# Latent queries, keys and values computed with tokens on partitions, heads turned by TensorE, and a new order of the portions between the heads

## What is computed

```python
q = (rmsnorm(c_q, g_cq) @ w_uq).reshape(B, S, MLA_HEADS, MLA_QK)          # 384 -> 8 heads x 96
kv = (rmsnorm(c_kv, g_ckv) @ w_ukv).reshape(B, S, MLA_HEADS, MLA_NOPE + MLA_V)   # 256 -> 8 x (64 + 64)
k_nope, v = kv[..., :MLA_NOPE], kv[..., MLA_NOPE:]
k = jnp.concatenate([k_nope, k_rope], axis=-1)       # k_rope: 32 features, the same for all heads
q = rmsnorm(q, g_qn)
k = rmsnorm(k, g_kn)
q = concat([q[..., :64], apply_rope_2(q[..., 64:], cos, sin)]); k likewise
return dense_attention(q * (MLA_QK ** -0.5), k, v)   # softmax over 256 keys
```

## Time and profile before

| | |
|---|---|
| median of 3 runs | 1648.69 us (1645.78 to 1649.99) |
| the profiled execution | 1644.55 us |
| its span | 1642.8 us |
| mean granted clock of TensorE in it | 0.995 |
| PE busy | 1589.0 us (97%) |
| DVE, ACT busy | 1129.8 us (69%), 919.0 us (56%) |

### The profile page before, as it was taken

The page is one execution under the profiler, slowest core; times in us unless marked ns, Lnnn a source line. Parts: engine busy times, 40 slices in busy tenths (PEclk is TensorE's granted clock), DMA queues, the critical chain, the costliest instruction groups (busy, mean ns, idle before and its releaser), DMA issues. The chain is left out here.

```text
span 1642.8 us, 31046 instructions
## 1 busy us (share of the span) xinstructions
PE 1589.0 (97%) x12874; PEld 1463.2 (89%) x12874; DVE 1129.8 (69%) x1763; ACT 919.0 (56%) x1459; POOL 127.2 (8%) x106
## 2 busy tenths in 40 slices
PE   6999999999999999999999999999999999999999
PEld 3987478999999999966899999878999998799999
DVE  2799677645566655897765556778887567788873
ACT  3444756545365444647554446767666467676662
POOL 0230000112001100300011000000101000001110
PEclk9999999999999999999999999999999999999999
DMA  9443666656546555435566653323555533245553
GB/s 395 160 152 131 258 236 227 235 216 240 192 167 221 205 188 201 155 125 207 195 228 237 220 184 119 118 78 130 207 191 202 204 112 116 77 137 200 207 193 118
DMA packets 46172, 303.36 MB, mean 185 GB/s; under 512 B 5072, under 2 KB 7376, under 8 KB 12752
## 3 DMA queue, kind: packets, MB, share of 16 engines
q1 hardware_dynamic: 45312, 299.78, 50.7%
q0 software_dynamic: 288, 0.92, 0.1%
q10 hardware_dynamic: 432, 0.68, 0.1%
HBM read 298.22 MB, written 3.15 MB: 183 GB/s over the span
## 5 line engine op out<-in xcount | busy, mean ns | idle before, releaser
L2002 DVE TENSOR_TENSOR wl<-raw,wh 128x1040 fp32r<-128x1040 f32 (+1 forms) x472 | 576.4, 1260 | 295.8 <-ACT wh L1759 229.9
L1759 ACT ACTIVATE wh<-raw 128x1040 fp32r<-128x1040 f32 (+1 forms) x472 | 466.5, 1031 | 195.5 <-PE bank L1552 109.3
L1547 PE MATMUL bank<-hx_hi,wh 128*128 128x256 f32 x1856 | 519.6, 280 | 6.0 <-ACT hx_hi L1759 3.8
L1552 PE MATMUL bank<-hx_lo,wh 128*128 128x256 f32 x1856 | 516.2, 278 | 0.0
L1550 PE MATMUL bank<-hx_hi,wl 128*128 128x256 f32 x1856 | 514.7, 277 | 0.3 <-DVE wl L2002 0.2
L1547 PEld LDWEIGHTS bank<-hx_hi,wh 128*128 128x128 f32 x1856 | 349.0, 188 | 10.8 <-issue 9.8
L1550 PEld LDWEIGHTS bank<-hx_hi,wl 128*128 128x128 f32 x1856 | 349.1, 188 | 2.8 <-issue 1.7
L1552 PEld LDWEIGHTS bank<-hx_lo,wh 128*128 128x128 f32 x1856 | 348.8, 188 | 1.0 <-DVE hx_lo L1995 0.4
L1550 PE MATMUL bank<-hid_hi,wl 128*128 128x256 f32 x912 | 252.2, 277 | 1.4 <-DVE wl L2002 1.4
L1547 PE MATMUL bank<-hid_hi,wh 128*128 128x256 f32 x912 | 252.5, 277 | 0.3 <-ACT wh L1759 0.2
L1552 PE MATMUL bank<-hid_lo,wh 128*128 128x256 f32 x912 | 251.9, 276 | 0.0
(11 more groups left out here) (218 smaller groups left out, 1891.5 us busy)
## 6 DMA issues: line engine op xcount, KB each, us to landing
raw<-in_wts SPq DMA_DIRECT2D x208, 1032.0 KB, 4.9
raw<-in_wts SPq DMA_DIRECT2D x50, 1024.0 KB, 6.6
raw<-in_wts SPq DMA_DIRECT2D x20, 776.0 KB, 4.3
raw<-in_wts SPq DMA_DIRECT2D x4, 584.0 KB, 4.4
tscr<-tmp SPq DMA_DIRECT2D x4, 512.0 KB, 7.4
bias<-tscr SPq DMA_DIRECT2D x4, 512.0 KB, 6.0
raw<-in_wts SPq DMA_DIRECT2D x2, 648.0 KB, 4.0
xTc<-in_ctxT SPq DMA_DIRECT2D x1, 1024.0 KB, 10.6
```

The source lines that it names most:

```text
L1547: pe.matmul(out, block(f, M.wh, w0 + k, ncols, c, m), x_hi, start=first and k == 0 and o == 0, stop=False, skip_group_check=True)
L1552: ins = pe.matmul(out, block(f, M.wh, w0 + k, ncols, c, m), x_lo, start=False, stop=last and k == nk - 1, skip_group_check=True)
L1759: return act.activation(out, in_, func, bias=bias, scale=scale)
L2002: tt(M.wl[k][:, cols], M.raw[r][:, cols], M.wh[k][:, cols].bitcast(F32), ALU.subtract).then_inc(*on.inc(lo))
```

## The change

Four parts, for both layers of the second block.

1. **Queries.** Tokens go on partitions: `mla_q` multiplies `cqn` (128 tokens, stationary) by `w_uq` (384 columns, four heads), nine matmuls for each of two token blocks and two halves of the heads: Q0, Q1 are the token blocks of heads 0 to 3, Q2, Q3 of heads 4 to 7. ACT squares 128x384 and copies the 64 plain features; DVE rotates the 32 others with short operations and sums the squares per head. The rest, `qn2`, is four transposes on PE (128x96 to 96x128), root on ACT, and a copy to `q2` with the gain.
2. **Keys and values.** `w_ukv` is stored with all key columns ahead of all value columns. K0, K1 are the two token blocks (six matmuls of 512 columns each). ACT squares 512 columns, DVE sums per head; the first rest (`mla_k2`) takes the root on eight columns and scales by four DVE products; it puts a second rest on `pending` (`mla_k3`: eight transposes, two copies to `k2` with the gain). V is as before, and is now what gives `ukv` back.
3. **Tables.** Sine and cosine are made as 128x32 and not 96x256, and twelve small operations (`rope_rows`) multiply the gains in. `swap2` and a column of constants go away, POOL's `lora1` memset too; the shared key part is turned by two 32-column transposes, rotated and its squares summed.
4. **The table of portions.**

```diff
-BETWEEN = ("h r D0 h L0 L2 N r r D2 D4 r D3", "", "D1 r r Q0", "K0", "", "s K1 h s V Q1", "r r", "s r D5 h h", "h r",
-           "Q3 Q2 h", "", "s K2 r r r K3 h", "s", "r O0 h O1 s", "", "O2", "", "h O3 h", "h", "h s T0 T1 T2 T3 h")
+BETWEEN = ("h r D0 h D2 r L0 r", "L2 N D4", "D3 r", "D1 r r K0", "s K1 r", "Q0 r r", "Q1 r r h h", "r D5 h", "V h",
+           "Q2 h h", "Q3 r h", "r O0 h", "O1 s", "h", "O2 h", "h", "O3 h", "h", "h", "h s T0 T1 T2 T3 h")
```

The core of the rest:

```diff
 TensorE
-    def qn2(s, s_free, r, r_free, sq, t_sq, xg, t_xg, t_s, t_r, **_):
-        for j in range(4):
-            ins = mm(s.t[:, j:j + 1], sq.t[0:96, P * j:P * j + P], M.ones[0:96, 0:1], j == 0, True)
-        mm(r.t[0:96, :], M.swap2[0:96, 0:96], xg.t[0:96, :], True, True).then_inc(*on.inc(t_r))
+    def mla_q(f, tb, b, free, cq_toks, t):
+        out, sl = b.t[:, 0:384], slice(P * tb, P * tb + P)
+        for k in range(3):
+            mm(out, M.cqn[0][:, k, sl], block(f, M.wh, k, 384, 0, 384), k == 0, False)
+            mm(out, M.cqn[0][:, k, sl], block(f, M.wl, k, 384, 0, 384), False, False)
+            ins = mm(out, M.cqn[1][:, k, sl], block(f, M.wh, k, 384, 0, 384), False, k == 2)
+    def heads_turned(o, y):
+        for i in range(4):
+            ins = pe.transpose(o.t[0:96, P * i:P * i + P], y.t[:, 96 * i:96 * i + 96], M.ident)
+    def mla_kv(f, c0, tb, b, ck_toks):
+        for k in range(2):
+            c = slice(1024 * k + c0, 1024 * k + c0 + 512)
+            mm(b.t[:, :], M.ckn[0][:, k, sl], M.wh[f["k"]][:, c], k == 0, False)
+            mm(b.t[:, :], M.ckn[0][:, k, sl], M.wl[f["k"]][:, c], False, False)
+            ins = mm(b.t[:, :], M.ckn[1][:, k, sl], M.wh[f["k"]][:, c], False, k == 1)
-    def mla_k2(sq, x, nb, nb_free, tn, **_):
-        mm(nb.t[0:96, :], M.ones[0:96, 0:96], sq.t[0:96, :], True, True).then_inc(*on.inc(tn))
+    def mla_k3(ys, ready, os, free, ts, **_):
+        for i in range(2):
+            heads_turned(os[i], ys[i]).then_inc(*on.inc(ts[i]))
 VectorE
+    def rope_on(dst, w, src, C, S, t):
+        tt(w[0], src, C, ALU.mult)
+        tt(w[1][:, :, 0:16], src[:, :, 16:32], S[:, :, 0:16], ALU.mult)
+        tt(w[1][:, :, 16:32], src[:, :, 0:16], S[:, :, 16:32], ALU.mult)
+        tt(dst, w[0], w[1], ALU.add)
+    def mla_k2(tb, b, d, ys, y_free, t_krr, t_r, t_y, **_):
+        for i in range(2):
+            tt(y[:, :, 0:64], b.t[:, T * i:T * i + T].rearrange("p (h c) -> p h c", c=64), r.to_broadcast([P, 4, 64]), ALU.mult)
+            tt(y[:, :, 64:96], M.krt[:, tb, :].unsqueeze(1).to_broadcast([P, 4, 32]), r.to_broadcast([P, 4, 32]), ALU.mult)
 Plan
+        def latent(part):
+            if not ukv:
+                ukv.append(take(("ukv", l), look=False))
+            t = mla_values(ukv[0]) if part == "V" else keys(int(part), ukv[0])
+            n_kv.append(t)
+            if len(n_kv) == 3:
+                p.done(ukv[0], t)
```

More of the change, by code:

```diff
@@ L85, in shape_constants @@
     c["swap1"] = j1
[L86 to L91, removed]
+    sq = np.concatenate([c[k] for k in ("ident", "ones", "bones", "swap1")], axis=1)
     t = np.arange(T)
@@ L218, in __init__ @@
         b1_off = cur[0]
-        self.ident, self.ones, self.bones, self.swap1, self.swap2 = (
-            cst[:, P * i:P * i + P] for i in range(5))
+        self.ident, self.ones, self.bones, self.swap1 = (
+            cst[:, P * i:P * i + P] for i in range(4))
         self.V = lambda k: vec[:, VT[k][0]:VT[k][0] + VT[k][1]]
@@ L1149, in tables @@
         t, t_l = ev("mm"), ev("tab")
-        t_d = [ev("tab") for _ in range(18)]
+        t_d = [ev("tab") for _ in range(19)]
         t_sin = [ev("sin"), ev("sin")]
@@ L1156, in tables, with rope_rows @@
         small["t_l"] = t_l
-        tmps.give(small["rb"], t_d[0], t)
-        tmps.give(angb, t_d[-1])
         tmps.give(kb, t_d[-1])
-        t_rope[:] = [t_sin[1]]
+        small.update(ang=angb, t_sin=t_sin, t=t)
+    def rope_rows():
+        t_g = [ev("tab") for _ in range(12)]
+        step("rope_rows", ang=small["ang"], rb=small["rb"], t_sin=small["t_sin"], t_rw=small["t_rw"], b1_free=b1_free,
+             t_g=t_g)
+        tmps.give(small["rb"], t_g[-1], small["t"])
+        tmps.give(small["ang"], t_g[-1])
+        t_rope[:] = [t_g[-1]]
     def copy_out(i):
@@ L1281, in lora_norm @@
             pending.append(rest)
-        q_toks, k_toks, v_toks, qs_toks = [], [], [], []
+        q_toks, k_toks, v_toks, qs_toks = [[], []], [[], []], [], [[], []]
         uq = []
[L1287 to L1294, removed]
@@ L1456, in rest @@
                 pending.pop(0)()
-        portion = {"r": rest, "s": p.one, "h": p.one_half, "V": lambda: mla_values(ukv[0])}
+        portion = {"r": rest, "s": p.one, "h": p.one_half, "V": lambda: latent("V")}
         portion.update({f"D{j}": (lambda j=j: hfree.update(x=[dil_piece(j)])) for j in range(6)})
@@ L1933, in lora2 @@
             fn(dst, us[c][0].t[:, 0:T], ACT.Copy).then_inc(*on.inc(c_toks[c][0]))
+        on.wait_ge(t_sw, y1_free)
+        fn(y1.t[:, 128:192], br.t[:, 0:64], ACT.Square).then_inc(*on.inc(t_k2))
     def mla_v(j, b, t, x, rf, **_):
@@ L2500 @@
     lams = np.stack([i[k] for k in ("lambda_q1", "lambda_k1", "lambda_q2", "lambda_k2")], axis=1)
+    rows = np.concatenate([np.float32(10000.0) ** (-np.arange(16, dtype=np.float32) / np.float32(16))]
+                          + [i[f"g_mla_{k}_2"][l][64:96] for l in range(2) for k in "qk"]).astype(np.float32)
     arrays = {
```

358 lines of the change are left out of this document (195 added, 163 removed).

## The result

| | before | after |
|---|---|---|
| median of the runs | 1648.3 us (4 runs, 1645.8 to 1650.0) | 1693.4 us (4 runs, 1692.4 to 1694.4) |
| ratio, 95% interval | 1 | 1.0275, 1.0257 to 1.0293 |
| span of the profiled execution | 1642.8 us | 1692.6 us |
| first head gemm to head 8's maximum, layers 0 and 1 | 81.06 and 81.06 us | 96.02 and 98.09 us |
| from there to the end of the last value product | 41.94 and 41.95 us | 49.50 and 49.91 us |

The kernel is 45 us slower; 1675 was forecast, with 1692 as the upper end. The direction and the place were right, the size was not. The two stretches of the table hold 47.5 of the 49.8 us by which the profiled spans differ (the profiled executions happen to be one of the shortest of before and the longest of after; the medians differ by 45.1). The other 2.4 lie ahead of them: the first head gemm starts at 996.1 instead of 993.7.

A forecast was written before the change was run, and what follows sets the result against it. PE was taken to bound the part up to head 8, a DVE and ACT ring to share in bounding the rest. Two layers at 13.2 us added 26.4 to 1644.55, plus 4.1 to the median: 1675 us, range 1637 to 1692.

The forecast's parts named there:

- Point 1: Before the first scores: the rest of D2's norm has no PE work behind it, so PE waits 2.4 us.
- Point 2: At the latent norm, behind D3's gemm (end z): it needs a bank D3 just filled, so PE waits 1.3 us.
- Point 3: Before D1's norm product: the latent block on DVE and ACT delays D1's square; PE waits 5.6 us, until z + 16.45.
- Point 4: Before scores(2): D1's chain of norms ends at z + 20.2, so PE waits 1.1 us.
- Point 5: At K0's turning: head 3's softmax, D5's split and K0's scaling come first, so PE waits 3.6 us.
- Point 6: Heads 3 to 5: head 3's transposes wait 1.6 us, Q1's wait 1.8; V ends at z + 51.4.
- Point 7: Before head 8: uq1's split must wait for V to free its buffer; head 8's maximum starts 13.2 us later.
- Behind it the ring rules: Behind head 8's maximum: the DVE and ACT softmax loop, 4.4 us a head with half a split, keeps today's 42 us.
- The wait of 5.6 us can bring one: At K0: one clock fall costing 1.7 us, hidden by PE's wait; nothing in the sum, four falls, 7 us, in the range.
- PE stays the bound: Rival at the latent block against D1: PE never waits there, so the kernel gets faster, 1624 or 1631 us; chance 0.20.
- the waits are half: Rival: 8.6 of 17.2 us of waits before head 8 fall away, and 4 behind it, giving 1650 us; chance 0.08.
- The clock falls again and again: Rival: four to eight clock falls of 1.7 us that matter add 7 to 14 us, 1682 to 1689; chance 0.07.

The follow-up runs named there:

- e12: New arithmetic under the same third table of portions as e13, plus idle products before scores(2), K0's turn, Q0's turn and scores(4); 1638.0 us, ratio 0.9943.
- e4: Changed kernel plus unread idle products (six, three, two, three, two) in five PE waits, sized to those waits; 1685.1 us, ratio 1.0233.
- e14: e11 plus idle products of 256 columns in its PE waits; 1674.2 us, ratio 1.0159.
- e11: Changed kernel with V moved behind K1's gemm and eight weight-split portions taken out between heads 8 and 16; 1682.3 us, ratio 1.0213.
- e13: Changed kernel with only another table: latent norm and D1 before the heads, V between heads 1 and 2, Q2 before head 7; 1640.3 us, ratio 0.9953.

## Why the prediction was wrong in size

**PE's work: nearly right.** 12.4 us a layer were worked out, 11 to 14 by the bounds, and 10.5 measured in e12, just under them; which term lacks the rest is not worked out. The query product of 384 columns starts every 0.175 us (seven intervals in 1.22, from 1062.28 to 1063.50), so 36 of them are 6.3, the middle that was taken:

```profile
1062.28 0.34 PE L1583 MATMUL bank<-wl,cqn_hi 128*128 128x384 f32 x1
...
1063.50 0.34 PE L1583 MATMUL bank<-wh,cqn_lo 128*128 128x384 f32 x1
```

**The walk to head 8: right, step by step.** Point 1: 2.4 forecast, 2.28 measured. Point 2: 1.3, and 1.42. Point 3: D3's gemm ended at 1036.5 (start of its last product plus one interval), which is z, and D1's norm product came at z + 16.5 against z + 16.45 in the walk, behind a wait of 5.25 against 5.6. Point 4: the wait of 1.1 before scores(2) did not come; K0's six products took 3.3 us at half clock and stood in its place. Point 5: 3.6 forecast, 2.94 measured. Point 6: head 3's transposes 1.6 and 1.77; Q1's 1.8 did not come, again with PE at half rate ahead of it. Point 7: head 8's maximum at z + 54 in the walk, z + 55.7 in the trace. The first part grew by 15.0 and 17.0 us where 13.2 was forecast. The sign "PE busy share about 75%" did not come, it was 85%: the records of products at half clock are longer, so the share hides part of the loss.

**The step that failed first:** "Behind it the ring rules", and "I take the 42 it has now, since it is the same ring". It took 49.5 and 49.9. It is not the same ring: in the new table 11 half splits are due behind head 8 where 7 were, among them the second half of uq1, of which point 7 had seen that it can't be made earlier. I had priced one turn (4.4 us with half a split in front) and never counted the turns. With the clock kept this part is still 45.1 and 45.5 (e4), and with V moved and the splits thinned out as well 38.7 and 37.8 (e14). How much of that is V's place and how much the splits is not taken apart with the clock kept.

**The step that failed second:** "The wait of 5.6 us can bring one, at K0, where PE waits anyway; so the sum has nothing for it and the range up to 1.7 for each of four falls". The reason given for K0 is right in kind, since e4 gives back 0.3 and 2.3 us of the first part. But it was carried over to the whole stretch, and behind head 8 e4 gives back 4.4 in each layer. Eleven stretches came instead of four at most, 58 us long in both layers together, nearly half of that time behind head 8. e4 measures 8.3 us for those of five waits, e14 8.1 on top of e11. The Trainium skill ("TensorE: Matmul & The Clock Gate", section "HAM oscillation — how this bites in real kernels") tells of a matmul loop that waits some 3 to 5 us for a transfer at each of its tiles, starts every next tile at half rate, and pays for that each time instead of once. The trace agrees on the repetition, with eleven stretches, and not on the length: stretches also began behind waits of 1.69 and 1.94 us. So it was an error to apply the rule to the two longest waits alone.

**The sum.** In the two stretches of each layer 26.4 us were forecast and 47.5 came. e4's stretches are 11.4 shorter than after's (4.7 and 6.7), which is the clock (in the two profiled executions; the medians are 8.3 apart). Of the remaining 9.7, 6.7 lie behind head 8, where e4 takes 45.1 and 45.5, and 2.9 ahead of it, where the walk was 1.5 a layer short. That e14 lands on 1674 does not mean that the forecast's 1675 was right: e14 also has V in another place, and its first part is 16 to 17 us longer than before's while the second is 3 to 4 shorter.

**The rivals.** "PE stays the bound" and "the waits are half" fell with the 5.25 us. "The clock falls again and again", with 0.07, was the nearest: its mechanism is shown, and it is one of two causes, but its 1682 to 1689 were too short as well. The cases had been set up as alternatives; the forecast case and this one happened together.

## What to carry to other kernels

When work moves between queues, count the operations that fall due in each part, not only the price of one turn of its loop: a portion that can do nothing where it is written comes back in a later part. Where PE is to wait more than once, set down a fall of the clock behind each wait as a term of the sum and not of the range, unless PE waits again right behind it; a few idle products in the bank that is overwritten next show within one run what the clock costs, if their price is read from a row of the same kind of product. A saving on the bound engine was worth nothing here until the order let it be reached: the same arithmetic stood at +2.8%, +1.1%, +0.1% and -0.6% under four tables, idle products included in the last.

## What was not expected of the hardware

- The granted clock fell behind waits shorter than the 3.16 us of the earlier trace rows: to 0.50 at 1132.52 behind a wait of 1.94, and at 1094.97 behind 0.62 and 1.69, with a little work between them. Behind the 2.28 before the first scores it stayed at 1.00 in layer 0 and fell in layer 1, for the same work: the same wait may or may not bring one.

```profile
1015.00:1021.00 6.00, 3.72 (x31) 3.31 (x31) 2.24 (x4) 2.09 (x5) 0.00 (x0) 1.00 0.41 162
1368.04:1371.45 3.41, 3.41 (x19) 3.41 (x18) 1.12 (x3) 2.13 (x6) 0.00 (x0) 0.50 0.00 0
```

- At half clock, the records of which those stretches are made start apart by 0.43 us for a latent product of 512 columns (0.234 at full clock), and the eight score records of two latent heads take 3.1 instead of 1.5 to 1.6.
- Matmuls whose result is never read count as work for the clock: in e12 no stretch at 0.50 is left in either layer, where e13, without them, has one in each.
